# Identity products in TensorE's waits, and some steps of the first mixer and of the attention moved

## The reference

```python
for i in range(2):                                    # first block
    h = rmsnorm(x, ln1_g[i]) @ w_in[i]
    x = x + concat(fox, diff, mla attention of h) @ w_o[i]
    up = causal_dwconv(rmsnorm(x, ln2_g[i]) @ w_up[i], conv_w[i], conv_b[i])
    x = x + (silu(up[..., :2816]) * up[..., 2816:]) @ w_down[i]
x = rmsnorm(x, final_g)
# second block: layer 0 an mLSTM (4 heads, two directions, latent and context tokens)
q, k, v, o, z, g = split(modulate(x) @ ml_w_in)       # g: the gates, 16 columns
h = mlstm(q, k, v, log_i, log_sigmoid(f))             # both directions, added
x = x + g_l * ((sigmoid(o) * head_rms(h) * silu(z)) @ ml_w_out)
# layer 1: windowed attention with a sink, 16 heads over 4 key groups, keys of latent and context
x = x + g_l * ((softmax(q k + band, sink) v * silu(z)) @ at_w_out)
```

## Time and profile before

| | |
|---|---|
| three runs, us | 2761.62, 2762.51, 2763.31; median 2762.51 |
| the profiled execution, us | 2760.68 |
| its span, us | 2759.0 |
| mean granted clock of TensorE, share of full | 0.968 |
| PE busy | 2545.1 us, 92% |
| DVE, ACT, POOL busy | 1173.5, 1020.9, 975.3 us |
| DMA | 200.58 MB, mean 73 GB/s |

### The profile page before, as it was taken

How to read it: one execution, slowest core, us unless ns; L and a number is a source line. 1 busy time by engine, 2 the same in 40 slices (tenths; PEclk the granted TensorE clock), 3 DMA queues, 4 the chain that set the end, 5 groups by cost and what they waited for, 6 DMA issues and landing times.

```text
span 2759.0 us, 33987 instructions
## 1 busy us (share of the span) xinstructions
PE 2545.1 (92%) x13182; PEld 2112.6 (77%) x13182; DVE 1173.5 (43%) x2127; ACT 1020.9 (37%) x1862; POOL 975.3 (35%) x519
## 2 busy tenths in 40 slices
PE   5998799999998979999989999989999998898888
PEld 4886688888787768888777778878777887786666
DVE  3356599510346559841251222410122242445564
ACT  4455444422455444443331322212132222354542
POOL 3332355755333145776522212223221223321121
PEclk9999999999999999999989999999999999899999
DMA  4211154322210235423311001111100111110000
GB/s 154 77 43 65 66 206 153 107 92 92 100 64 33 77 111 195 137 96 107 109 39 46 16 24 46 65 50 54 54 16 24 39 64 60 57 62 25 30 24 31
DMA packets 54015, 200.58 MB, mean 73 GB/s; under 512 B 5984, under 2 KB 5984, under 8 KB 52960
## 3 DMA queue, kind: packets, MB, share of 16 engines
q1 hardware_dynamic: 51696, 188.65, 20.1%
q10 hardware_dynamic: 2160, 9.76, 1.0%
HBM read 196.29 MB, written 2.10 MB: 72 GB/s over the span
## 4 chain that ended last, share of the span: by engine, by line
PE 82%; DVE 7%; ACT 4%; POOL 4%; issue 3%; DMA 0%; ACTq 0%; DVEq 0%; POOLq 0%
PE ps L528 51%; PE ps L548 14%; PE ps L578 7%; PE ps L866 5%; POOL wl L2273 2%; PE ps L723 1%; POOL norm_acc L2286 1%; PE ps L1060 1%; DVE norm_sq L1699 1%; ACT wh L1097 1%; PE ps L739 1%; POOL norm_sq L2387 0%; PE ps L873 0%; PE ps L1045 0%; PE ps L1044 0%
## 5 line engine op out<-in xcount | busy, mean ns | idle before, releaser
L2273 POOL TENSOR_TENSOR wl<-wring,wh 128x1024 fp32r<-128x1024 f32 (+1 forms) x305 | 761.7, 2497 | 1379.4 <-ACT wh L1097 1367.4
L1097 ACT ACTIVATE wh<-wring 128x1024 fp32r<-128x1024 f32 (+1 forms) x305 | 316.7, 1042 | 724.7 <-PE ps L528 717.7
L528 PE MATMUL ps<-hh,wh 128*128 128x512 f32 x1136 | 446.0, 393 | 20.7 <-DVE hl L1711 16.0
L528 PE MATMUL ps<-hl,wh 128*128 128x512 f32 x1136 | 444.6, 391 | 0.0
L528 PE MATMUL ps<-hh,wl 128*128 128x512 f32 x1136 | 444.4, 391 | 0.0
L528 PEld LDWEIGHTS ps<-hh,wh 128*128 128x128 f32 x1136 | 215.1, 189 | 69.6 <-DVE hl L1711 15.0
L528 PEld LDWEIGHTS ps<-hh,wl 128*128 128x128 f32 x1136 | 214.8, 189 | 45.6
L528 PEld LDWEIGHTS ps<-hl,wh 128*128 128x128 f32 x1136 | 215.1, 189 | 43.0
L548 PE MATMUL ps<-hh,wh 128*128 128x512 f32 (+1 forms) x472 | 200.6, 425 | 6.1 <-DVE hl L2254 3.4
L578 PE MATMUL ps<-arena 128*128 128x64 f32 (+2 forms) x720 | 183.6, 391 | 14.8 <-ACT arena L1317 5.6
L1736 DVE CUSTOM_DVE_ANT_0 arena<-arena 128x1024 f32<-128x1024 f32 x96 | 186.3, 1940 | 9.0 <-DVE arena L1925 0.8
(11 more groups left out here) (288 smaller groups left out, 5062.9 us busy)
## 6 DMA issues: line engine op xcount, KB each, us to landing
wring<-wts SPq DMA_DIRECT2D x290, 512.0 KB, 3.5
arena<-wts SPq DMA_DIRECT2D x48, 512.0 KB, 4.3
wring<-wts SPq DMA_DIRECT2D x16, 384.0 KB, 2.9
xL<-xt SPq DMA_DIRECT2D x1, 2048.0 KB, 9.6
arena<-tab SPq DMA_DIRECT2D x1, 2048.0 KB, 16.8
arena<-cv ACTq DMA_DIRECT2D x2, 1024.0 KB, 4.8
arena<-tab ACTq DMA_DIRECT2D x1, 2048.0 KB, 9.0
out_t<-xL ACTq DMA_DIRECT2D x8, 256.0 KB, 2.0
```

The lines of the kernel that those rows point to most:

```text
L528: mm = nc.tensor.matmul(o[0], a, b, start=start and k == first and j == 0, stop=stop and k == last and j == 2)
L1097: nc.scalar.activation(wh[:, sn % SPLIT_SLOTS, :kn * w], raw(u)[:, :kn * w], ACT.Copy).then_inc(act_done, tick("act", ("hi", u)))
L2273: G.tensor_tensor(wl[:, sn % SPLIT_SLOTS, :kn * w], raw(u)[:, :kn * w], wh[:, sn % SPLIT_SLOTS, :kn * w].bitcast(F32), ALU.subtract).then_inc(
```

## The change

- `stir(b, n)` on PE waits for the bank's last reader and then multiplies the identity by itself n times into 128 columns of bank b, which nobody reads. It stands ahead of and behind some norms, ahead of the second tile's transposes in `head_pv` (6 products; the branch with 15 is never reached, since t ends at NA-1), and ahead of the wait for `gl`.
- The weights of the gates come behind the first half of head 0's query and key weights, in the order of units and on ScalarE and GpSimd. PE does head 0's context queries ahead of the gates' context part, and ScalarE splits `("mqk", 0, 1)` and copies the first two tiles of `mqk` ahead of the gates' softplus. VectorE's final-norm scaling of `xL` moves from ahead of the gates to behind their transposed copy.
- ScalarE splits both halves of `("up", l, 1)` one place earlier: the first ahead of the root of ln2, the second alone at m = 0.
- The transposes of a head's last tile (`last_rows`) move: for heads 0 and 2 behind the decay rows of the next head, for heads 1 and 3 between z and o of the first `oz` unit, which are done as whole products, z first, with both halves given back at the end.
- The chain of value products `apv` is cut after its second product; the rest follows in the next step, behind its scores and transposes.

```diff
@@ -86,11 +86,12 @@
                 add(("dn", l, j, c), "w_down", l, sum(FF_CHUNKS[:c]), FF_CHUNKS[c], [(256 * j, 256)])
-    add(("gate",), "ml_w_in_2", 0, 0, KT,
-        [(ML_G, 4), (None, 28), (ML_G + 8, 4), (None, 28), (ML_G + 4, 4), (None, 28), (ML_G + 12, 4)])
     for f in range(2):
...
             add(("mqk", h, 0), "ml_w_in_2", 0, 0, KT, [(256 * h, 256)])
+            if h == 0:
+                add(("gate",), "ml_w_in_2", 0, 0, KT, [(ML_G, 4), (None, 28), (ML_G + 8, 4), (None, 28),
+                                                       (ML_G + 4, 4), (None, 28), (ML_G + 12, 4)])
             add(("mqk", h, 1), "ml_w_in_2", 0, 0, KT, [(1024 + 256 * h, 256)])
@@ -578,6 +579,14 @@
+            def stir(b, n):
+
+                if b in readers:
+                    reader = readers.pop(b)
+                    pe.wait_ge(sems[reader[0]], at(*reader))
+                for _ in range(n):
+                    nc.tensor.matmul(ps[:, b, 0:128], idn, idn, start=True, stop=True)
+
             def norm(tag):
@@ -593,7 +602,11 @@
             for l in range(DEPTH):
+                if l:
+                    stir(7, 10)
                 norm(("ln1", l))
+                if l:
+                    stir(6, 13)
@@ -764,7 +777,9 @@
                     out_part(2, m, (2 + m) % 8)
+                stir(7, 21)
                 norm(("ln2", l))
+                stir(6, 13)
@@ -799,15 +814,16 @@
                 pe.wait_ge(dve_done, at("dve", "hl", ("mC", 0), m))
-            claim([4, 5], "dve", "glf")
-            product(ps[0:100, 4, 256:512], rows(gate_all, *hc), [gate_unit])
-            norm(("mL", 0))
             for i in range(2):
...
                             stop=u is query_units[1])
+                if u is query_units[0]:
+                    norm(("mL", 0))
+            claim([4, 5], "dve", "glf")
+            product(ps[0:100, 4, 256:512], rows(gate_all, *hc), [gate_unit])
             norm(("fin", 0))
@@ -848,12 +864,19 @@
+            def last_rows(h, b):
+
+                pe.wait_ge(pool_done, at("pool", "hn", h, NA - 1))
+                claim([b], "act", "ht", h, NA - 1)
+                for j in range(4):
+                    last = nc.tensor.transpose(ps[:, b, 128 * j:128 * j + 128],
+                                               hb[:, (NA - 1) % 2, 128 * j:128 * j + 128], idn)
+                last.then_inc(pe_done, tick("pe", ("ht", h, NA - 1)))
+
             def head_pv(h):
-                for t in range(NA + 1):
+                for t in range(NA):
                     for d in range(2):
-                        if t == NA:
-                            break
                         b = 4 + 2 * d
@@ -867,6 +890,8 @@
                     if t:
+                        if t in (1, NA):
+                            stir(3, 15 if t == NA else 6)
                         pe.wait_ge(pool_done, at("pool", "hn", h, t - 1))
@@ -886,6 +911,8 @@
                     chain(ps[:, b + 1, :], [(pick, mmx[0:36, TC:TA])], ("mb", h, d))
+                if h % 2:
+                    last_rows(h - 1, 0)
                 for j in range(2):
@@ -911,9 +938,20 @@
                     b = 4 * (j % 2)
-                    claim([b, b + 1], "act", "sgo", j)
+                    if j > 8 * f:
+                        claim([b, b + 1], "act", "sgo", j)
                     claim([b + 2, b + 3], "dve", "zz", j)
+                    if j == 8 * f:
+                        us = views(("oz", j))
+                        product(ps[:, 2, 256:512], rows(side(1), *hc), us)
+                        product(ps[:, 3, :], lat(side(1)), us, ("z", j))
+                        last_rows(h, 4)
+                        claim([b, b + 1], "act", "sgo", j)
+                        product(ps[:, 0, 256:512], rows(side(0), *hc), us)
+                        product(ps[:, 1, :], lat(side(0)), us, ("o", j), *[("used", x[0]) for x in us])
+                        continue
                     project(("oz", j), both(b // 2, P, side(0), ("o", j)) + both(b // 2 + 1, P, side(1), ("z", j)))
+                stir(0, 20)
                 pe.wait_ge(dve_done, at("dve", "gl", 8 * f + 7))
@@ -929,8 +967,10 @@
+            stir(0, 20)
             norm(("mL", 1))
             norm(("mC", 1))
+            stir(1, 6)
@@ -1060,15 +1100,18 @@
                     last.then_inc(pe_done, tick("pe", ("at", u)))
-                if s >= 7 and s % 4 == 3:
+                if s >= 7 and s % 4 in (3, 0):
                     n = (s - 7) // 4
                     g, i = divmod(n, 4)
-                    pe.wait_ge(act_done, at("act", "apt", 4 * n + 3))
-                    pe.wait_ge(dve_done, at("dve", "apt", 4 * n + 2))
-                    claim([6], "dve", "ag3", n)
-                    chain(ps[:, 6, :], [(atv[:, t, 128 * (g // 2):128 * (g // 2) + 128],
-                                         apt[:, n % 2, k].rearrange("p h b -> p (h b)"))
-                                        for k, t in enumerate(keys_of(i))], ("apv", n))
+                    pairs = [(atv[:, t, 128 * (g // 2):128 * (g // 2) + 128],
+                              apt[:, n % 2, k].rearrange("p h b -> p (h b)")) for k, t in enumerate(keys_of(i))]
+                    if s % 4 == 3:
+                        pe.wait_ge(act_done, at("act", "apt", 4 * n + 3))
+                        pe.wait_ge(dve_done, at("dve", "apt", 4 * n + 2))
+                        claim([6], "dve", "ag3", n)
+                        chain(ps[:, 6, :], pairs[:2], ("apv0", n), stop=False)
+                    else:
+                        chain(ps[:, 6, :], pairs[2:], ("apv", n), start=False)
                 if s < nu:
@@ -1330,13 +1373,16 @@
                     square(("ln2", l), m, ("xo", l, 2))
+                split(("up", l, 1), first)
                 root(("ln2", l))
...
                 for m in range(2 * FT + 1):
-                    if m % 2 == 0 and m < 2 * FT:
+                    if m == 0:
+                        split(("up", l, 1), second)
+                    elif m % 2 == 0 and m < 2 * FT:
                         split(("up", l, m // 2 + 1) if m < 2 * FT - 2 else ("dn", l, 0, 0))
@@ -1389,14 +1435,23 @@
                         square_both(2 * j + 1)
-            split(("mqk", 0, 0), first)
             square_both(6)
             square(("mL", 0), 7, ("xd", DEPTH - 1), fgn[:, 7:8])
-            split(("mqk", 0, 0), second)
+            split(("gate",))
             square(("fin", 0), 7, ("xd", DEPTH - 1))
...
             root(("fin", 0))
+            split(("mqk", 0, 1))
+
+            def take_qk(h, m):
+
+                act.wait_ge(pe_done, at("pe", "mqk", h, m))
+                nc.scalar.activation(mqk[:, m, :], psf[:, 1024 * (m % 2) + 256:1024 * (m % 2) + 1024],
+                                     ACT.Copy).then_inc(act_done, tick("act", ("mqk", h, m)))
+
+            take_qk(0, 0)
+            take_qk(0, 1)
@@ -1437,17 +1492,17 @@
                         act.wait_ge(pe_done, at("pe", "ht", h, t - 1))
+                        b = t % 2 if t < NA else 4 * (h % 2)
                         nc.scalar.activation(hn[:, 4 * (h % 2):4 * (h % 2) + 4, 128 * (t - 1):128 * t],
-                                             ps[:, t % 2, :].rearrange("p (a b) -> p a b", a=4), ACT.Copy).then_inc(
+                                             ps[:, b, :].rearrange("p (a b) -> p a b", a=4), ACT.Copy).then_inc(
                             act_done, tick("act", ("ht", h, t - 1)))
...
                 for m in range(4):
-                    if m % 2 == 0:
+                    if m % 2 == 0 and h + m:
                         split(("mqk", h, 1) if m == 0 else ("mv", h, 0))
-                    act.wait_ge(pe_done, at("pe", "mqk", h, m))
-                    nc.scalar.activation(mqk[:, m, :], psf[:, 1024 * (m % 2) + 256:1024 * (m % 2) + 1024],
-                                         ACT.Copy).then_inc(act_done, tick("act", ("mqk", h, m)))
+                    if h or m > 1:
+                        take_qk(h, m)
                 if h == 0:
@@ -1944,7 +1999,7 @@
             scaled_split(("mL", 0), lambda m: fgn[:, 8 + m:9 + m], hH, hLo, 0)
-            scaled(("fin", 0), lambda m: col("fin", m), xL)
+            dve.wait_ge(act_done, at("act", "rstd", ("fin", 0)))
             V.memset(mvt[:, :, 512:514], 1.0).then_inc(dve_done, tick("dve", ("vones",)))
@@ -1986,6 +2041,7 @@
             dve.wait_ge(dve_done, now("dve"))
+            scaled(("fin", 0), lambda m: col("fin", m), xL)
```

7 lines of the change are left out of this document (3 added, 4 removed).

## The result

Four runs of the changed kernel, the profiled one among them, took 2712.89 to 2723.32 us, median 2720.03, against 2762.07 for the kernel before: a ratio of 0.9843 with a 95% interval of 0.9831 to 0.9854. Four later runs took 2712.72 to 2720.11, ratio 0.9833 (0.982 to 0.9846). The median of all eight is 2718.55. The prediction was 2717, range 2702 to 2731. The profiled execution took 2712.89, 47.8 us less than the profiled one of before (2760.68), where 45.7 were forecast. It is the fastest of its four runs: the medians differ by 42.0 us, with all eight runs by 43.5, so what is read off this pair of profiles comes out some 4 us high.

The account below looks back on a forecast made before the run. TensorE was taken to bound the kernel, through its waits and lower clock. Terms 0.8+3.4+0.6+9.0+8.4+9.6+10.4+3.5 = 45.7 us off the profiled 2760.68 gave 2715, and 2717 for the median; range 2702 to 2731.

Parts of the forecast that it names:

- What bounds it: Whole kernel: 82% of the chain is TensorE; time is won only where it waits or multiplies at the lower clock.
- Identity products cost nothing: Norms, heads, output products: 181 products at 0.22 us each fit inside existing waits, cost nothing and hold the clock.
- rival with 0.53 us for each: Identity products to one bank don't overlap; from 0.53 us a product they outweigh all gains: 2767, chance 0.03.
- rival that they don't (2726.5): Identity products don't hold the clock, so 0.8+3.4+0.6 and 2x(0.95+1.5) us are lost: 2726.5, chance 0.14.
- last norms: Identity products at the last norms win 0.95 us on the norm pair, taken as 0.6 us.
- up(1): At ln2, earlier weights remove the 2.38 us wait, less 0.3; with identity products 4.5 us per layer, 9.0 in all.
- rival of the early subtraction: GpSimd's early subtraction for up(1) holds up VectorE's norm scaling, at most 2.40 us per layer: 2722, chance 0.04.
- Gates: First head's query weights and copies ahead of the gates cut the 10.04 us wait to 2.7: 8.4 us won.
- Last rows: Last head rows move behind the next work: heads 0 and 2 win 9.6 us, heads 1 and 3 10.4.
- Value chain: Attention: cutting each value chain in two issues the next scores earlier; 3 or 4 places counted, 3.5 us won.
- rival (2730): Split value chain costs time, as VectorE's gating waits for the second part: 10 us lost, 3.5 not won, chance 0.09.
- Heads 1 and 3: Last rows between z and o: 7.2 us won against a new wait of about 2.2; net 5.2 each, 10.4 in all.

Follow-up runs that it names:

- bettered kernel: Changed kernel with attention's first key weights split earlier, first oz half given back earlier, identity products added at gates, rows, in attention and ahead of its last products: 2694.78 us.
- oz earlier: Changed kernel with o of each half's first oz unit going through the first half of the weights first, so that half comes back earlier: 2717.48 us.
- more identity products: Changed kernel with 12 identity products added at the gates, and 5 and 2 around the last rows of heads 0 and 2: 2719.82 us.

## Why the prediction was right, and where its steps were not

- **What bounds it.** Right. TensorE's gaps and its slow time explain the result: the identity products took 42.7 us of the gaps of the kernel before, which wins nothing by itself, the waits got shorter by another 21.1 (186.0-122.2-42.7), and half of the fall in busy slow time, (123.7-70.7)/2, is 26.5; 47.6 in all, against 47.8.
- **Identity products cost nothing.** Right: behind each of their 14 groups a wait of 0.44 to 1.3 us stays. (The six in a head stand ahead of the first tile's transposes, not the second's.) The rival with 0.53 us for each is out: 0.23. They hold the clock: right at the norms and output products, 9.3 us when they are taken out, 9.7 forecast. The rival that they don't (2726.5) is out. At the last norms, where I took 0.6, the two profiles read -0.2 and 0.9. But the 9.7 are theirs only in the company of the earlier weights; alone they give 4.2. My sum treated the terms as free of each other. Removed one at a time, the five parts cost 9.3 + 7.5 + 9.7 + 26.1 + 2.1 = 54.7 us, and all together gave 43.5. All five are taken from the same 2718.55, so 2 us of error in it makes 8 us of that difference; the dependence is shown by the wait at ln2, not by this sum.
- **up(1).** Mechanism right, size right only for the pair of edits: I priced the wait at the 2.38 us of the kernel before, while with the identity products in front of it, it would have been 3.7. The rival of the early subtraction is out: with the early weights and no identity products TensorE waits 3.70 us for the first scaled tile, as before the change. In the profile of the changed kernel GpSimd subtracts from 325.41 to 327.76, and VectorE's first scaling begins at 327.86, when the root is done (327.83). They miss each other by 0.1 us here. By the Trainium skill (SBUF — State Buffer, Who interferes with whom) the two engines block each other only while both run.
- **Gates.** 7.9 read, 9.7 by removal, 8.4 forecast. The wait and the time of the scans were right within 0.3 us. The 1.06 us behind ScalarE's copy of the second part was missed, and so was the slow stretch of 3.4 us, by which the 96 products ended at +21.0 us, not +19.2.
- **Last rows.** The waits came out to a tenth. What was sized wrong is the clock: I expected a new fall of 6.8 us behind each of heads 0 and 2, and took 2 us off for it; 3.41 came, so 1.0 us each was taken off too much. These stages gave 1.6 us beyond the forecast.
- **Value chain.** The term that failed most: 3.5 forecast, 6.5 to 7 us of waits found, since I counted the 3 or 4 places with a wait of 1.24 in the earlier trace rows and not the waits of 1.60 and 1.46 us at 2664.6 and 2713.6 of the trace of before, which went as well (the one behind them grew from 0.53 to 1.18). The rival (2730) had its first step right: in the changed kernel VectorE's gating waits for the second part 13 times, 21.4 us in all and 2.7 at most. But except for that one wait TensorE's didn't grow, so it is out.
- **Left out altogether:** the waits of 0.52 and 0.90 us at the end of the up products (1.9 us given back), and short slow stretches elsewhere, which cost the profiled run 1.9 us more than the one of before. Together 3.8, which nearly undid the 5.3 that the attention gave beyond its term. That the sum came so close is thus partly luck: two errors of 4 to 5 us of opposite sign. Besides, the median lies 3 us (1.5 by all eight runs) above the forecast, less than the spread of the runs, so no closer agreement can be claimed.
- **Slips in the sum.** Heads 1 and 3 are 7.2-2.2 = 5.0 each by their own terms, not 5.2; a split of 1.0 and a subtraction of 2.40 are 3.4, not 3.6; the rival at 2726.5 is 2717+9.7 = 2726.7. None of them matters.

## What to carry over

- When an engine's clock falls after waits, price a wait at its length and half of the slow stretch behind it, and look at what can be put into it first: other due work is best (the last rows, 26 us), and products that nobody reads are next, as long as they end before the wait does.
- Edits on either side of one wait are not independent. After making one part of a path faster, read the next wait as it will be then, not as it is: 2.38 us became 3.7, and the early split of the weights was worth 7.5, not 4.2.
- Where runs of one kernel spread by 10 us with the clock, a gain of 4 us shows in the gaps of a trace long before it shows in the median. Judge small edits by their waits, and in company: three worth 1.1, 5.9 and 0 us alone were worth 19.6 together, though part of that is where the clock happened to fall.

## What the runs showed of the hardware that I had not expected

The slow stretches are not fixed to the waits behind which they stand. With the same gaps of 32.0 or 32.1 us, TensorE was busy at the lower level in the attention for 22.4 to 36.0 us, and in edits that leave the attention alone. Filling the waits at three places ahead of it made four slow stretches go, and others came (2136.70, 2338.08), where the changed kernel had none; and with the same waits filled, the bettered kernel had two of the four again.

Yet the series isn't arbitrary. Counted from the first score, the slow stretches begin at the same points in three profiles, the second of the changed kernel and those with the gates and with up(1) at their old place: at 26.7, 57.5, 125.7, 197.4 and 286.2 us. In three others, with the last rows at their old place, with oz earlier and with more identity products, they begin at 55.6, 96.5, 127.3, 168.2, 202.3 and 291.1 us, each within 0.2 us and with the same lengths. In all it is 34.1 us at the lower level in the first three and 45.5 in the other three. These kernels differ only ahead of the attention, and the first profile of the changed kernel, with the same program as the second, has a series of its own. So the series recurs to 0.2 us under different code, differs under the same code, and is set by something other than the attention and its waits. What that is isn't settled: where the program stands when it gets there would fit, but no run here varies that alone.
